# Sixteen query-weight slots, weight copies one batch late, value rows dealt 6, 12 and 8, and the last rows split by columns in a decoder-layer kernel

## The reference, cut to what matters

```python
def peer_ffn(h, w_query, sub_keys, expert_u, expert_v):
    q = (h @ w_query).reshape(B, S, PEER_HEADS, 2, PEER_HALF)            # 8 heads
    scores = jnp.einsum('bshcd,hckd->bshck', q, sub_keys)
    ...                                                                   # top 16 of 16 x 16 pairs
    idx, gate = ...                                                       # 16 experts a head and token
    def chunk_fn(args):                                                   # 128 tokens, 128 experts each
        xc, ic, gc = args
        u = jnp.take(expert_u, ic, axis=0)
        act = gelu(jnp.einsum('ckd,cd->ck', u, xc))
        vv = jnp.take(expert_v, ic, axis=0)
        return jnp.einsum('ck,ckd->cd', gc * act, vv)
...
return rms_norm(h + peer_ffn(...), final_norm)
```

## Time and profile before

| | us |
|---|---|
| median of 3 runs | 2054.76 |
| runs | 2054.68, 2054.76, 2059.27 |
| the profiled execution, its own time | 2051.57 |
| its span in the trace | 2049.5 |

### The profile page before, as it was taken

The page is one execution under the profiler, slowest core; times in us unless marked ns, Lnnn a source line. Parts: engine busy times, 40 slices in busy tenths (PEclk is TensorE's granted clock), DMA queues, the critical chain, the costliest instruction groups (busy, mean ns, idle before and its releaser), DMA issues.

```text
span 2049.5 us, 21545 instructions
## 1 busy us (share of the span) xinstructions
PE 1791.2 (87%) x7539; PEld 1189.9 (58%) x7539; DVE 1364.9 (67%) x2203; ACT 559.9 (27%) x1010; POOL 1028.1 (50%) x643
## 2 busy tenths in 40 slices
PE   7999999999999999655655677888878899999997
PEld 7998998888998898522222233333334444444442
DVE  4372453223333348799999988888888767888865
ACT  5344453345434510201000032232315530000001
POOL 5343343444432313566565545555555556878732
PEclk9999999999999999888888799999999999999999
DMA  8975455665535689899999999999999989999997
GB/s 210 244 172 137 149 181 164 190 192 186 170 126 185 190 308 405 331 421 418 416 418 417 411 413 405 401 406 409 402 418 366 364 320 394 387 407 391 399 421 292
DMA packets 157651, 647.42 MB, mean 316 GB/s; under 512 B 25895, under 2 KB 31087, under 8 KB 95599
## 3 DMA queue, kind: packets, MB, share of 16 engines
q0 software_dynamic: 73728, 450.98, 54.6%
q1 hardware_dynamic: 83824, 195.16, 29.6%
HBM read 729.91 MB, written 2.10 MB: 357 GB/s over the span
## 4 chain that ended last, share of the span: by engine, by line
PE 61%; DMA 19%; DVE 15%; issue 3%; POOL 1%; ACT 0%; DVEq 0%; POOLq 0%; ACTq 0%; SPq 0%
PE acc L1739 8%; DMA v_high<-in_peer_v_dram,idx 8%; PE misc L1705 8%; PE misc L1739 8%; DMA u_ring<-in_peer_u_dram,idx 5%; DVE product L1274 5%; PE acc L1396 5%; PE acc L1398 5%; PE acc L1397 5%; PE acc L1403 5%; PE acc L1405 5%; PE acc L1404 5%; DVE product L1276 5%; DMA v_low<-in_peer_v_dram,idx 3%; PE acc L1733 2%
## 5 line engine op out<-in xcount | busy, mean ns | idle before, releaser
L465 POOL TENSOR_TENSOR w_lo<-raw,w_hi 128x1024 fp32r<-128x1024 f32 x112 | 273.3, 2441 | 428.6 <-ACT w_hi L562 428.3
L1705 PE MATMUL misc<-v_high,diag 128*128 128x512 f32 x512 | 272.0, 683 | 102.7 <-DMA v_high<-in_peer_v_dram,idx 87.2
L1705 PE MATMUL misc<-v_low,diag 128*128 128x512 f32 x512 | 272.5, 685 | 99.0 <-DMA v_low<-in_peer_v_dram,idx 82.0
L562 ACT ACTIVATE w_hi<-raw 128x1024 fp32r<-128x1024 f32 x224 | 237.0, 1060 | 352.5 <-PE acc L1405 171.4
L870 DVE TENSOR_TENSOR w_lo<-raw,w_hi 128x1024 fp32r<-128x1024 f32 x112 | 148.8, 1329 | 267.0 <-ACT w_hi L562 266.8
L505 POOL DMA_INDIRECT u_ring<-in_peer_u_dram,idx x160 | 209.5, 1309 | 194.7 <-DVE dots L1276 137.9
L1705 PEld LDWEIGHTS misc<-v_high,diag 128*128 128x128 f32 x512 | 106.8, 218 | 256.5 <-issue 133.1
L1396 PE MATMUL acc<-t_hi,w_hi 128*128 128x256 f32 x896 | 255.3, 285 | 0.0
L1398 PE MATMUL acc<-t_hi,w_lo 128*128 128x256 f32 x896 | 253.5, 283 | 0.0
L1397 PE MATMUL acc<-t_lo,w_hi 128*128 128x256 f32 x896 | 253.5, 283 | 0.0
L1705 PEld LDWEIGHTS misc<-v_low,diag 128*128 128x128 f32 x512 | 107.3, 219 | 251.0 <-issue 130.9
(11 more groups left out here) (249 smaller groups left out, 2648.9 us busy)
## 6 DMA issues: line engine op xcount, KB each, us to landing
u_ring<-in_peer_v_dram SPq DMA_DIRECT2D x48, 1024.0 KB, 8.8
raw<-in_w_in_dram SPq DMA_DIRECT2D x64, 512.0 KB, 5.2
raw<-in_xattn_wk_dram SPq DMA_DIRECT2D x32, 512.0 KB, 4.8
raw<-in_xattn_wv_dram SPq DMA_DIRECT2D x32, 512.0 KB, 3.9
raw<-in_w_out_dram SPq DMA_DIRECT2D x32, 512.0 KB, 4.5
raw<-in_xattn_wq_dram SPq DMA_DIRECT2D x32, 512.0 KB, 4.6
raw<-in_xattn_wo_dram SPq DMA_DIRECT2D x32, 512.0 KB, 4.5
praw<-in_peer_wq_dram SPq DMA_DIRECT2D x32, 512.0 KB, 8.7
```

The costliest lines, as they stand in the source:

```text
L465: nc.gpsimd.tensor_tensor(w_lo[:, j % RING, :, :], raw[:, j % RING, :, :], w_hi[:, j % RING, :, :].bitcast(F32), ALU.subtract).then_inc(lo ...
L1705: ins = nc.tensor.matmul(o, diag[:, n % 4, :], v_slot(n % VS)[:, i * CW:(i + 1) * CW], start=False, stop=False)
```

## The change

1. **Query slots.** `SLOTS` goes from 12 to 16. The four new ones (`praw_first`) lie in the room of `t2_lo`, which is free once the "q" product is done. SP loads query chunks 0 to 3 into them between the chunk loads of item 1 of "o" (two raw chunks, one query chunk, four times). The other 28 follow as before; chunk c from 16 on waits for `peer_used` of c - 15, where it was c - 11. The first gathers of `expert_v` into `v_low`, which shares that room, and into `v_high` wait for 20 and 32 used chunks, where only `v_high` waited, for 24.
2. **Copies one batch late.** At batch b ACT does `key_one_hots(b + 1)` and then `weights_T(b - 1)`. The last batch of each half is copied at the end of period 13 and of period 15.
3. **Value rows.** Periods 8 to 13 take 12 rows each, and 14 and 15 take 8 each (11 each before).
4. **Last rows.** Of rows 112 to 123 of the second half PE takes the odd ones (6). Row 124 is DVE's. Rows 125 to 127 are shared: PE takes columns 0 to 511 (one matmul), DVE the columns 512 to 2047. Before row 125 DVE adds PSUM's columns 512 to 2047 to its sum (`take_sums`), and PE takes DVE's columns 0 to 511 by a matmul with the identity. The last row is added by DVE in three parts, and ACT squares each as it comes and reads the first 512 columns from PSUM.
5. **First half's output.** Its sums, its product with the gain and its scaling, which DVE did in one go before row 112, are done before rows 112, 115 and 117.

```diff
-    SLOTS = 3 * RING
-    praw = put("praw", [P, SLOTS, KC, CW], F32, at_raw)
+    SLOTS = 4 * RING
+    praw = put("praw", [P, SLOTS - RING, KC, CW], F32, at_raw)
+    praw_first = put("praw_first", [P, RING, KC, CW], F32, at_t2 + 16 * KB)
...
         def by_pe(m):
-            return m >= LATE and m % 2 == 1
+            return LATE < m < SHARED - 1 and m % 2 == 1
...
-            at = FIRST_V + 6 * (PH - 2) + 11 * (p - PH)
-            return range(at, min(at + 11, TILE0))
+            if p < GROUPS - WHOLE:
+                return range(FIRST_V + 36 + 12 * (p - PH), FIRST_V + 48 + 12 * (p - PH))
+            return range(TILE0 - 8 * (GROUPS - p), TILE0 - 8 * (GROUPS - p - 1))
...
+            sp.wait_ge(chunk_used, n0 * CH)
+            for c in range(RING):
+                item(n0 + 1, w_o_r, 1, chunks=range(2 * c, 2 * c + 2))
+                query_chunk(c)
+            with sp.Fori(2, items) as i:
                 item(i + n0, w_o_r, i)
             n0, items = ITEMS["peer"]
-            for c in range(PC):
-                i, j, u = c // CH, c % CH, c % SLOTS
-                if c < RING:
-                    sp.wait_ge((lo_even, lo_odd)[u % 2], n0 * HALF + (u // 2 - 1))
+            for c in range(RING, PC):
+                if c < 2 * RING:
+                    sp.wait_ge((lo_even, lo_odd)[c % 2], n0 * HALF + (c % RING // 2 - 1))
                 elif c < SLOTS:
-                    sp.wait_ge(chunk_used, n0 * CH - HALF + (u % RING + 1))
+                    sp.wait_ge(chunk_used, n0 * CH - HALF + (c % RING + 1))
                 else:
                     sp.wait_ge(peer_used, c - SLOTS + 1)
...
                     for b in scatters(p, k):
                         if (b + 1) % BATCHES:
                             key_one_hots(b + 1)
-                        weights_T(b)
+                        if b % BATCHES:
+                            weights_T(b - 1)
+                if p in (GROUPS - WHOLE - 1, GROUPS - 1):
+                    weights_T(BATCHES - 1 if p < GROUPS - 1 else 2 * BATCHES - 1)
...
+            def take_sums():
+                dve.wait_ge(v_used, TILE0 + BY_PE)
+                dve.wait_ge(v_added, added_before(SHARED))
+                step(nc.vector.tensor_tensor(y_sum[:, 1, CW:], acc[:, :, :, :].rearrange("p a b c -> p (a b c)")[:, CW:], y_sum[:, 1, CW:], ALU.add))
+
+            def add_last():
+                m = TILE0 - 1
+                dve.wait_ge(late_landed[late_slot(m)], 16 * (m // V2S + 1))
+                dve.wait_ge(v_added, added_before(m))
+                for i in range(1, 4):
+                    cols = slice(i * CW, (i + 1) * CW)
+                    nc.vector.scalar_tensor_tensor(y_sum[:, 1, cols], v_slot(late_slot(m))[:, cols], low_wts[:, PH + m // TOP, m % TOP:m % TOP + 1],
+                                                   y_sum[:, 1, cols], ALU.mult, ALU.add).then_inc(y_added, 1)
...
                 if m == LATE:
-                    finish(0)
-                if not by_pe(m):
+                    first_sums()
+                if m == LATE + 3:
+                    gained(0)
+                if m == LATE + 5:
+                    scaled(0)
+                if m == SHARED:
+                    take_sums()
+                if m == TILE0 - 1:
+                    add_last()
+                elif not by_pe(m):
                     add_values(m)
...
-            for m in range(LATE + 1, TILE0 - 1, 2):
+            for m in range(LATE + 1, SHARED - 1, 2):
+                take_late(m).then_inc(v_used, 1)
+            pe.wait_ge(v_added, added_before(SHARED))
+            nc.tensor.matmul(high[0], ident[:, :], y_sum[:, 1, 0:CW], start=False, stop=False)
+            for m in range(SHARED, TILE0 - 1):
                 take_late(m).then_inc(v_used, 1)
             take_late(TILE0 - 1).then_inc(y_done, 1)
```

More of the change, by code:

```diff
@@ L368, in late_slot, with high_bank @@
             return (m + 4) % V2S
+        def high_bank(i):
+            return acc[:, i // 2, i % 2, :]
         def score_batch(b):
@@ L854, in _ @@
             act.wait_ge(wts_ready, GROUPS)
-            for m in range(LATE + 1, TILE0, 2):
-                if m == LATE + 5:
-                    finish(0)
+            for m in range(LATE + 1, LATE + 6, 2):
                 late_diagonal(m)
-            finish(1)
+            squares_0()
+            scaled(0)
+            for m in range(LATE + 7, SHARED - 1, 2):
+                late_diagonal(m)
+            for m in range(SHARED, TILE0):
+                late_diagonal(m)
+            squares_1()
+            scaled(1)
         @block.vector
@@ L1712, in take_late @@
                 pe.wait_ge(diag_ready, n + 1)
-                for i, o in enumerate(high):
-                    ins = nc.tensor.matmul(o, diag[:, n % 4, :], v_slot(late_slot(m))[:, i * CW:(i + 1) * CW], start=False, stop=m == TILE0 - 1)
+                for i, o in enumerate(high if m < SHARED else high[:1]):
+                    ins = nc.tensor.matmul(o, diag[:, n % 4, :], v_slot(late_slot(m))[:, i * CW:(i + 1) * CW], start=False,
+                                           stop=m in (SHARED - 2, TILE0 - 1) and (i > 0 or m >= SHARED))
                 return ins
```

85 lines of the change are left out of this document (53 added, 32 removed).

## The result

The changed kernel takes 2040.66 us (median of 6 runs, 2038.35 to 2042.55), beside 2055.01 us for the kernel before in the same comparison (6 runs, 2049.75 to 2059.27). The ratio is 0.993 with a 95% interval of 0.9916 to 0.9945: 14.4 us faster, where 21 were forecast. The profiled execution took 2039.45 us with a span of 2037.5, against a span of 2049.5 before. By the profiles the gain is therefore only 12.0 us; the rest of the 14.4 is that the profiled execution of before lay 3.4 us under its median, and that of after 1.2 us under its own. There is one trace of each kernel, and the profiled executions lie from 3.4 us under (before) to 5.5 us above (e8_noskip) the median of their kernel's runs, so a difference of a few us between two traces proves little by itself.

What follows compares the result with a forecast made beforehand. It took full DMA to bound the kernel from the query stage on, PE the last two periods, and a chain behind the last row's landing the end. 4.5 + 10.5 + 2.5 + 3.5 = 21.0 us off 2054.76 gave 2034, range 2027 to 2047.

Steps and rivals of the forecast that it cites:

- the signs that would have made the forecast wrong: Periods 8 to 13 over 62 us, last two periods' DMA share under 0.93, or PE waiting in item 1 of "o".
- Part 1, 4.5 us: Query stage: four chunks loaded earlier take 2.1 MB off a full DMA; 4.5 us, between nothing and 7.9.
- The shift is kept to the end: After the query stage: as all that follows is full DMA, the 4.5 us won there stay won.
- Parts 2 and 3, 10.5 us: Last two periods: PE's 16.0 us of waits and six rows go, less the rows' 9.4 us elsewhere; 10.5 us.
- rival B: Periods 8 to 13: a row costs more than 1.57 us; at 2.6, part 3 loses 6, total 2040; chance 0.15.
- 57 + 56 = 113 us: Periods 14 and 15: together 113 us for what took 133.9, a gain of 20.9 before the rows' price.
- Rival C: Last two periods stay as long as DMA, DVE and POOL want; rows' price eats the copies' half; 2046; chance 0.10.
- The gap, 2.5 us: After the last dot product: tiles start at once, 2 us, and POOL's 7.14 us stall is split, 0.5; between 0 and 5.
- The tail, 3.5 us: Last landing to reduction: 4.1 to 4.2 us instead of 7.7; gain 3.5, between 2 and 4.
- A: Query stage: something else, DVE's own work, takes the chunks' room; slots give nothing; 2038; chance 0.14.
- D: Periods 8 to 13: waiting value rows hold expert rows in POOL, DMA runs dry; at 5.5 us a period 2067; chance 0.05.
- E: Last two periods: DVE delays POOL's issuing, 0.5 us more for each of 48 gathers, 24 us; 2058; chance 0.02.

Runs made afterwards that it cites:

- e8_noskip: Changed kernel, but gathers of first-half value rows 112 to 127 also fetch the zero-weight dense experts' rows; 2048.52 us, ratio 0.9972.
- e1_slots: Kernel before the change with only the sixteen query slots added; 2050.45 us, ratio 0.9985.
- e10_copies_rows: Kernel before the change with the late copies and value rows 6, 12, 8 together, nothing else; 2047.27 us, ratio 0.9966.
- e9_tiles_wait: Changed kernel, but the first three tile loads wait for the last dot product; 2041.09 us, ratio 0.9934.

## Why the prediction was right or wrong

The direction and the range held; the size was two thirds by the medians (14.4 of 21), 12.0 by the profiles. By the profiles, 9 of 21 us failed to come, in two of the four terms. Of the signs that would have made the forecast wrong none came: periods 8 to 13 took 60.5 us each, the DMA share of the last two is 110.9 / 117.3 = 0.95, and item 1 of "o" shows no wait of PE.

**Part 1, 4.5 us: mechanism right, size rather 3.** Period 1 ends 4.6 us earlier. The signs came as stated: the last query chunk is issued at 782.1, and `gate_exp(2)` on ACT's timeline:

```profile
849.30 0.31 ACT L763 ACTIVATE exps<-best,neg_best 128x16 f32<-128x16 f32 x1 [18.58 <-DVE neg_best L1254]
```

is 4.6 us earlier than in the earlier trace rows, and waits 6 us less. DVE's waits for gathered rows in 780 to 850 are 2.2 us where the earlier trace rows has 7.9. Item 1 of "o" took the four chunks with PE busy all 60.00 us. The size has a spread of its own: period 1 ends at 859.5 to 863.1 in the nine kernels with the slots, at 863.6 to 864.8 in the five without. The means, 860.9 and 864.1, are 3.2 us apart, which is what the runs of e1_slots gave; a single pair of traces shows anything from 0.5 to 5.3, so the 4.6 of this pair is partly luck. "The shift is kept to the end" is not borne out by the traces of e1_slots.

**Parts 2 and 3, 10.5 us: mechanism right, size wrong; 6.0 by the profile, 7.0 by e10_copies_rows.** The price of a row was 1.57 us in the forecast and 10.6 / 6 = 1.77 in the run, 1.2 us in all: rival B's direction, but far from its 2.6. The step that failed is the length of the last two periods, "57 + 56 = 113 us". The 111 us of busy DMA in it came out at 110.9. What failed is the reasoning from there: that with PE out of the way only small bubbles would be left. Period 15 of after is not full, since POOL issues its last gather 24 us before the period's end and the queue then runs empty, in the end at 27 GB/s; only the first tile loads fill in. The rows of before had shown this already, at the earlier trace rows: 0.87 in the last period. I had put all of its 9 us of idle DMA on PE's lateness, and it is 5.7 us with PE on time. The second sign of it was also missed: in period 14 the DMA is at 0.99 and DVE and PE still wait for gathered rows, and it moves 392 GB/s, not the 417 of periods 2 to 7. A share of 0.99 doesn't say that the bytes come at the best rate: e8_noskip has 421 in the same period, with the skipped rows fetched.

A second step failed beside it: "so ACT's diagonals are ready when PE wants them", which was to remove 16.0 us. The waits of 0.96 us behind the scatters went, and DVE's for `hotB`, but five others make up 13.6 us, four of them of 2.7 to 4.6, where the earlier trace rows has fifteen. Two pieces of ACT's timeline and two of PE's, all of after, say why:

```profile
1559.79 0.31 ACT L763 ACTIVATE exps<-best,neg_best 128x16 f32<-128x16 f32 x1 [6.00 <-DVE neg_best L1254]
...
1571.45 2.45 ACT L795 ACTIVATE hotA<-keys,listsT 96x128 f32<-96x128 f32 x8 [3.37 <-PE acc L1807]
...
1575.27 0.39 ACT L771 ACTIVATE diag<-ident,low_wts 128x128 f32<-128x128 f32 x1
...
1564.42 5.21 PE L1778 MATMUL misc<-v_high,diag 128*128 128x512 f32 x8 [4.61 <-ACT diag L771]
...
1575.80 6.34 PE L1778 MATMUL misc<-v_low,diag 128*128 128x512 f32 x8 [2.66 <-ACT diag L771]
```

The copy no longer waits for PE, but `key_one_hots(b + 1)` ahead of it does, since its `hotA` buffer is free only when PE has done scatter b - 1; and the next diagonal stands behind both. The longest wait stands behind `gate_exp`, which waited 6.0 us for DVE's routing. What these waits cost the kernel is not shown: the DMA share is 0.99 beside them. Rival C held in part: it had the last two periods kept long by their DMA.

**The gap, 2.5 us: wrong; nothing was gained.** The landing came 2.0 us later behind period 15 than in before, which is within the scatter of that stretch (374.1 to 378.3 in the kernels without part 4). The tiles were to start within 5 us of the last dot product and started after 10.0, for another reason than before: not because PE was behind, but because the last value row was late. And where experiments made them start after 4.8 or 6.2 us, the landing didn't move. The step that failed is "with PE no longer behind, tiles loaded meanwhile start at once", and beside it the assumption that a start of PE is worth anything in a stage which is at 0.98 of the DMA's share. The stated reason against it was in the forecast itself ("DMA ends last"), and should have put the term at zero. The split of POOL's stall, 0.5 of it, gave nothing that can be measured either.

**The tail, 3.5 us: right; 3.6.** DVE, PE and ACT behind the last landing:

```profile
2027.04 1.13 PE L1787 MATMUL acc<-v_more,diag 128*128 128x512 f32 x2 [1.33 <-DMA v_more<-in_peer_v_dram,idx]
2027.76 2.08 DVE L1364 SCALAR_TENSOR_TENSOR y_sum<-v_more,low_wts,y_sum 128x512 f32<-128x512 f32 x3
2028.20 0.60 ACT L837 ACTIVATE junk<-acc 128x512 bf16<-128x512 f32 x1 [9.12 <-PE acc L1787]
...
2029.75 0.69 DVE L1379 TENSOR_TENSOR y_out<-y_sum,final_gain 128x512 f32<-128x512 f32 x1
...
2030.35 0.69 DVE L1381 TENSOR_TENSOR y_out<-acc,final_gain 128x512 f32<-128x512 f32 x1
...
2031.07 0.16 DVE L1388 TENSOR_REDUCE ss<-sq 128x1 f32<-128x4 f32 x1
```

The four column parts run side by side: PE has its one 1.13 us after the landing, DVE its three at 2.8, ACT starts its first square at 1.16, and the reduction starts 4.0 us after the landing (4.2 forecast), where it was 7.6.

The same shortfall can be read off the DMA alone. From period 13 to the last landing, before had 508.7 us with 0.96 x 64.42 + 0.87 x 69.43 + 0.98 x 374.8 = 489.6 busy (with period 14 from its start at 1526.77), so 19.1 idle. After has 494.2 with 59.3 + 51.6 + 369.4 = 480.3 busy, so 13.9 idle. The shares are rounded to a hundredth, so each idle time is good to 2.5 us. The forecast had the idle time down to 2 in the two periods and 5.5 in the late stage. It is 6.3 and 7.5.

**The rivals.** A (slots give nothing) was wrong by e1_slots. B and C were each partly true. D asked for more than 4.5 us per period besides the 1.57 per row; what came is 0.2 us per row. E asked for 0.5 us more per gather; in period 14 a gather takes 35.18 / 24 = 1.47 us of POOL's busy time, against 1.36, in period 15 26.54 / 18 = 1.47 against 31.22 / 21 = 1.49, and the DMA share beside the first is 0.99. But an issue is slower beside a busy DVE: in the late stage of after it takes POOL 1.00 us while DVE is idle and mostly 2.15 or more beside DVE's row additions:

```profile
1653.49 1.00 POOL L533 DMA_INDIRECT v_last<-in_peer_v_dram,idx  x1 [0.30 <-issue]
...
1670.33 2.15 POOL L533 DMA_INDIRECT v_low<-in_peer_v_dram,idx  x1 [0.30 <-issue]
...
1656.08 2.35 DVE L1348 SCALAR_TENSOR_TENSOR y_sum<-v_more,low_wts,h 128x2048 f32<-128x2048 f32 x1 [5.79 <-DMA v_more<-in_peer_v_dram,idx]
...
1669.26 4.81 DVE L1348 SCALAR_TENSOR_TENSOR y_sum<-v_high,low_wts,y_sum 128x2048 f32<-128x2048 f32 x2
```

The Trainium skill's rule on the shared port ("SBUF — State Buffer", SBUF: two separate sides) is about such a delay. Whether it is at work here is not shown: DVE is idle mostly when few gathers are outstanding, so the filled queue could be the reason too. Nor is a cost to the kernel shown, as the DMA share of the stage is 0.98. The limit of 358 GB/s that the Trainium skill gives for a core's reads ("DMA: Bandwidth & Descriptors", Specifications) is passed again: slices of 417 to 421 GB/s stand in the page of after.

## What to carry to other kernels

When a full DMA is fed by one in-order queue of gathers, look for the time at which the last gather before a change of stage is issued: between that and the end of the period the share was 0.76 in after (1626.3 to 1650.1), and removed engine waits came back in part as waits for data. Take a stretch's gain as the idle time of the resource that stays full, less what the queue's running empty costs, and read GB/s beside the share. When a wait is to be removed, follow the engine's whole order: what else stands ahead of the instruction that was late, and what does that wait for? A term for starting an engine earlier was worth nothing here, where transfers end last. And hold one trace of a kernel against another only for differences larger than what traces of one kernel differ by.

## What the runs showed of the hardware that I had not expected

While a queue of gathers runs empty, the DMA can fall to 27 or 28 GB/s, one sixteenth of the 437 that it moves when full, for 2 us (after, 1644 to 1646) up to 7 us (e9_tiles_wait, 1638 to 1645). A gather issued as the last took 27.17 us to land in after and 29.78 in e8_noskip. e9_tiles_wait shows that this happens with nothing but gathers outstanding, and e8_noskip that rows skipped in a gather aren't what makes PE wait for it. Which engine lags, and why, is open. Skipped rows of a gather keep the DMA's share up and lower its rate: period 14 moves 392 GB/s at 0.99 with them and 421 at 1.01 without. Issuing a gather of the late stage takes POOL 1.00 us beside an idle DVE and mostly 2.15 or more beside DVE's additions of rows; the reason is open.
